# The first two up-projection units of an FFN, block by block in two PSUM banks, where a residual sum becomes the FFN's input

## The reference

```python
def rmsnorm(x, g):
    xf = x.astype(jnp.float32)
    y = xf * lax.rsqrt(jnp.mean(xf * xf, axis=-1, keepdims=True) + RMS_EPS)
    return (y * g.astype(jnp.float32)).astype(x.dtype)

def swiglu(h, w_gate, w_up, w_down):
    return (jax.nn.silu(h @ w_gate) * (h @ w_up)) @ w_down

def second_block(x, norm_g, ...):
    h = x
    for layer in range(DEPTH_2):
        g = norm_g[layer]
        u = rmsnorm(h, g[0])
        m = mixer_fox_nsa(u, ...) if layer % 2 == 0 else mixer_pool(u, ...)
        h = h + rmsnorm(m, g[1])
        u = rmsnorm(h, g[2])
        h = h + rmsnorm(swiglu(u, ffn_w_gate[layer], ffn_w_up[layer], ffn_w_down[layer]), g[3])
    return h
```

## Time and profile before

| | us |
|---|---|
| median of 3 runs | 1926.87 |
| the three runs | 1917.62, 1926.87, 1940.65 |
| span of the profiled execution, first to last instruction | 1930.8 |
| TensorE busy in it | 1849.1 (96%) |
| VectorE busy | 832.7 (43%) |
| ScalarE busy | 687.0 (36%) |
| mean granted TensorE clock | 0.949 |

### The profile page before, as it was taken

The page is one execution under the profiler, slowest core; times in us unless marked ns, Lnnn a source line. Parts: engine busy times, 40 slices in busy tenths (PEclk is TensorE's granted clock), DMA queues, the critical chain, the costliest instruction groups (busy, mean ns, idle before and its releaser), DMA issues.

```text
span 1930.8 us, 22596 instructions
## 1 busy us (share of the span) xinstructions
PE 1849.1 (96%) x8378; PEld 1431.2 (74%) x8378; DVE 832.7 (43%) x1244; ACT 687.0 (36%) x1124; POOL 30.4 (2%) x86
## 2 busy tenths in 40 slices
PE   8899889999999999999998899999998899999996
PEld 6576677888878887666666778888886678888885
DVE  3444256777743342321223354444323654444323
ACT  4533335444422223443334343332222633333221
POOL 1000000000000200000000000000002000000000
PEclk9999699999999998896897999999999899999998
DMA  4111022223332431000000212223321022223221
GB/s 156 55 44 44 22 79 83 100 87 107 104 105 86 109 111 34 12 23 11 23 23 11 88 56 97 98 98 110 105 90 66 22 73 93 96 98 114 102 78 43
DMA packets 37761, 142.72 MB, mean 74 GB/s; under 512 B 4496, under 2 KB 4656, under 8 KB 37440
## 3 DMA queue, kind: packets, MB, share of 16 engines
q1 hardware_dynamic: 36288, 138.43, 21.1%
q0 software_dynamic: 688, 2.31, 0.6%
q10 hardware_dynamic: 720, 1.10, 0.2%
HBM read 139.72 MB, written 2.10 MB: 73 GB/s over the span
## 4 chain that ended last, share of the span: by engine, by line
PE 90%; DVE 5%; ACT 3%; issue 2%; DMA 0%; DVEq 0%; ACTq 0%
PE ps L1301 25%; PE ps L1302 24%; PE ps L1303 24%; PE ps L1590 4%; PE ps L1626 3%; PE ps L1602 2%; DVE x L962 1%; DVE hlo L945 1%; PE ps L1426 1%; ACT hhi L549 1%; PE ps L1533 1%; DVE mt L956 1%; PE ps L1675 1%; PE ps L1706 1%; PE ps L1391 1%
## 5 line engine op out<-in xcount | busy, mean ns | idle before, releaser
L1301 PE MATMUL ps<-hhi,whi 128*128 128x512 f32 x1520 | 623.2, 410 | 40.7 <-DVE hlo L945 24.0
L1302 PE MATMUL ps<-hlo,whi 128*128 128x512 f32 x1520 | 600.5, 395 | 0.0
L1303 PE MATMUL ps<-hhi,wlo 128*128 128x512 f32 x1520 | 600.2, 395 | 0.0
L821 DVE TENSOR_TENSOR wlo<-raw,whi 128x1024 fp32r<-128x1024 f32 (+1 forms) x240 | 313.4, 1306 | 585.4 <-ACT whi L446 582.9
L446 ACT ACTIVATE whi<-raw 128x1024 fp32r<-128x1024 f32 (+1 forms) x240 | 269.4, 1122 | 621.9 <-PE ps L1303 621.6
L1301 PEld LDWEIGHTS ps<-hhi,whi 128*128 128x128 f32 x1520 | 290.7, 191 | 127.0 <-issue 42.5
L1303 PEld LDWEIGHTS ps<-hhi,wlo 128*128 128x128 f32 x1520 | 290.4, 191 | 62.7
L1302 PEld LDWEIGHTS ps<-hlo,whi 128*128 128x128 f32 x1520 | 290.9, 191 | 61.0 <-issue 6.4
L1301 PE MATMUL ps<-ahi,whi 128*128 128x512 f32 x528 | 209.5, 397 | 0.2 <-DVE wlo L821 0.2
L1303 PE MATMUL ps<-ahi,wlo 128*128 128x512 f32 x528 | 209.3, 396 | 0.0
L1302 PE MATMUL ps<-alo,whi 128*128 128x512 f32 x528 | 209.3, 396 | 0.0
(11 more groups left out here) (244 smaller groups left out, 1343.2 us busy)
## 6 DMA issues: line engine op xcount, KB each, us to landing
raw<-w_up_b SPq DMA_DIRECT2D x88, 512.0 KB, 3.5
raw<-w_up_a SPq DMA_DIRECT2D x44, 512.0 KB, 3.5
raw<-w_down_b SPq DMA_DIRECT2D x32, 704.0 KB, 4.0
raw<-w_in_b SPq DMA_DIRECT2D x23, 512.0 KB, 3.5
raw<-w_down_a SPq DMA_DIRECT2D x16, 704.0 KB, 3.9
raw<-w_in_a SPq DMA_DIRECT2D x19, 512.0 KB, 3.4
raw<-w_out_a SPq DMA_DIRECT2D x8, 512.0 KB, 3.5
raw<-w_out_b SPq DMA_DIRECT2D x8, 512.0 KB, 3.4
```

The lines of the kernel that those rows point to most:

```text
L821: dve.tensor_tensor(wlo[n % SPL][:, 0:cols], raw[n % RAW][:, 0:cols], whi[n % SPL][:, 0:cols].bitcast(f32), ALU.subtract).then_inc(lo_done, 1)
L1301: pe_.matmul(out, wh, hi, start=start, stop=False)
L1302: pe_.matmul(out, wh, lo, start=False, stop=False)
L1303: return pe_.matmul(out, wl, hi, start=False, stop=stop)
```

## The change

At `up_b0` and `up_b1` TensorE takes units 0 and 1 together: for each block k it waits for the operand, does the three products of unit 0 into bank 0, the three of unit 1 into bank 1, and then the square sum of the block. Both units signal `unit_done` behind their last block, unit 0 three products ahead of unit 1, and the last square sum follows. Ahead of the first block it now waits for the split weights of both units. The other phases, the other engines and the number of instructions of each kind are as before.

```diff
+            def two_units(p, e):
+
+                for k in range(KD):
+                    operand_ready(p, k)
+                    for u in range(2):
+                        last = block_mm(p, u, k, u, k == 0, k == KD - 1)
+                        if k == KD - 1:
+                            last.then_inc(unit_done, 1)
+                    squares(e, k)
+
             def gemm(p):
@@
                     e = RSTD_OF.get(p)
+                    if p in ("up_b0", "up_b1") and u < 2:
+
+                        if u == 0:
+                            pe_.wait_ge(lo_done, n + 2)
+                            two_units(p, e)
+                        return
```

## The result

| | before | after |
|---|---|---|
| median of 22 runs | 1925.18 us | 1937.88 us |
| lowest and highest | 1903.34, 1943.79 | 1918.53, 1954.39 |
| ratio | | 1.0078, 95% interval 1.0047 to 1.011 |
| profiled execution: span (own time) | 1930.8 | 1952.3 (1954.01) |

The ratio compares only the fast runs (those within 1.5% of the fastest run of the same kernel), so it isn't the ratio of the two medians (1.0066). The change makes the kernel slower by 0.8%, some 15 us, with an interval of 9 to 21 us; the medians lie 12.7 us apart. The two profiled spans are 21.5 us apart, and half of that is not the change's: 11.1 us lie ahead of the first boundary, where both programs are the same. What the change does is read from the boundaries alone.

The account below looks back on a forecast made before the run. TensorE, with 90% of the chain, was taken as the bound. Boundaries +6.3 us (a 4.4 us gain already in it) and clock +3.9 make +10.2 on 1926.87, stated as 1937.0 us; range 1925 to 1950, 8 times in 10.

Parts of the forecast that it names:

- Which chain is uncovered: Both boundaries, behind the last square sum: Ln, Exp, table load and two splits lose their cover; TensorE pauses 5.07 us.
- The blocks: TensorE at both boundaries: six products and a square sum take 2.23 us per block, with no wait between blocks.
- The second boundary's first part: First product to last square sum, 1538.78 to 1558.5: 17.8 us of blocks, 0.13 weight load, 1.75 for the low clock.
- The price of the clock: Behind the new pause at each boundary: the clock falls, costing 1.95 us each, +3.9 us for two.
- the clock is left alone: Rival, behind the new pauses: the clock does not fall, so only +6.3 us, 1933.2; chance 0.1.
- It stays low long after both pauses: Rival, behind both new pauses: the low clock costs 6.8 us in all, so +13.1 us, 1940.0; chance 0.15.
- The sum: Whole kernel: +6.3 us from both boundaries and +3.9 us from the clock, +10.2 us or 0.5%.
- The absolute time: Whole kernel: three-run median of 1926.87 us plus 10.2 us, stated as 1937.0 us.
- One reading: First FFN, kernel before: with two more table loads, unit 2's first product starts 6.3 us after the square sum ends.
- ScalarE held back by the square sums: Rival, operand ring at the boundaries: six squares held 0.6 us each and TensorE too, +3.6 us a boundary; chance 0.03.
- The Trainium skill's drain: Table-set switch in the uncovered chain: a rule adding about 1380 ns, making the sum about 2.8 us more.

Follow-up runs that it names:

- e1: The changed kernel with ScalarE's split of unit 2's weights put ahead of Ln, Exp and the table load: 1934.47 us against 1917.45, ratio 1.0073; boundaries 27.56 and 27.32 us.
- e2: The changed kernel with each block's square sum ahead of its six products: boundaries 31.89 and 30.92 us, pause 3.77 us.
- e3: The changed kernel with five unread products of ones with x put behind the last square sum to fill the pause: boundaries 31.21 and 30.46 us.
- e4: The kernel before, with only the split of unit 2's weights put ahead of Ln, Exp and the table load: boundaries 27.48 and 27.51 us.
- e7: The kernel before with the change made at the second boundary alone: boundaries 27.50 and 33.34 us.
- e8: The kernel before under another name, same instructions: ratio 1.0035 (0.9985 to 1.0085); boundaries 27.49 and 27.47 us.
- e6: Against the kernel before, three blocks of unit 1 put between unit 0's blocks, ScalarE's order unchanged: boundaries 28.29 and 27.75 us.

## Why the prediction was right

- **Which chain is uncovered** was right. Pause 5.16 us at both boundaries, forecast 5.07; e1 and e2 shortened it by the order alone, e3 left it and filled it.
- **The blocks** were right: 2.25 us apart, forecast 2.23, and no wait between them. From the first product to the end of the last sum the first boundary took 20.5 us (1121.93 to 1142.46), forecast 20.35.
- **The second boundary's first part** was too short in the sum: 21.1 us (1554.14 to 1575.27) against 19.7. The low clock lasted until about 1560.3, 6.2 us behind the first product, not 3.5. It is no cost of the change, for it lasts differently long in each execution. But the changed order pays for it, and the old order doesn't. In the old order a boundary has a length of 27.47 to 27.51 us in all seven cases of four profiles (before, e4, e7, e8), with slow stretches (the time at the low clock behind the first product) from 3.5 to 5.8 us, since its waits for `hlo` absorb the difference. In the changed order half of the slow stretch goes into the time. The windows over the first 8 us of a boundary, both of the changed kernel and the second of e3, give the slow stretch as (1 - clock) x 16 us:
```profile
1121.93:1129.93 8.00, 8.00 (x21) 0.69 0.00 0
1554.14:1562.14 8.00, 8.00 (x19) 0.61 0.01 2
1553.71:1561.71 8.00, 8.00 (x25) 0.79 0.01 2
```
(these rows have TensorE alone: length, busy time, clock, DMA share, GB/s), and from the start of unit 2 (us behind the first product) less half of it the same is left each time, to 0.1 us:

| changed order | slow stretch | start of unit 2 | less half the slow stretch |
|---|---|---|---|
| changed, first | 5.0 | 25.67 | 23.2 |
| changed, second | 6.2 | 26.28 | 23.2 |
| e3, first | 5.0 | 25.68 | 23.2 |
| e3, second | 3.4 | 24.94 | 23.3 |
| e7, second | 3.5 | 25.04 | 23.3 |

The prediction knew that half of the slow stretch is lost, and took the stretches of one profile, 4.8 and 3.5 us, as fixed.
- **The price of the clock** behind the new pause was 1.5 and 1.8 us, 3.3 in all, for 3.9 forecast. Over all pauses of this study in which the clock fell it was 1.5, 1.8, 1.7, 1.7 (e2) and 2.8 us (e7), with a mean of 1.9, so the forecast of 1.95 us each was right in its size; how much a single pause costs it could not tell. The rival "the clock is left alone" is out. "It stays low long after both pauses", at 3.4 us each, didn't happen in the profile after, but at the one pause of e7 2.8 us of the 3.4 did.
- **The sum**: +6.3 + 3.9 = +10.2 forecast, +11.3 at the boundaries, +15 (9 to 21) in whole times. Of the 11.3, 3.3 are the clock behind the pause (e3), and some 8 the pause less the gain ahead of it, 1.4 of them the slow start of the second boundary. The whole times alone would not have told the forecast from its rival of +13.1; the boundaries do.
- **The absolute time** was luck in part: 1937.0 forecast and 1937.88 measured. The forecast stood on a median of three runs of the kernel before; its median was 1925.18 in the 22 runs here, and 1917.45, 1928.25 and 1922.18 in the later comparisons, so a hit within 1 us means nothing.
- **One reading** was wrong and cost nothing: at the first FFN not two more table loads lie behind the square sum, but one. ScalarE loads at 297.63 and at 299.57; the third load of that stage, at 291.56, is over before the square sum ends. The 6.35 us there are the 5.07 of this chain and one more load of 1.28, so the row bears the forecast of the pause out better than the prediction said.
- **ScalarE held back by the square sums**: it was, by 1.0 to 1.3 us at each of six squares of the first boundary and up to 1.8 at the second, and TensorE never waited for it. That rival is out.
- **The Trainium skill's drain** behind a table load ("ScalarE: Activation LUTs", "What ACT_TABLE_LOAD costs") isn't in the trace after either: the load starts at 1143.85 and the split at 1145.14. With the page's 1380 ns of drain the pause would have been about 6.5 us, an estimate from the page's figure; it was 5.16.

## What to carry to other kernels

Work that looks like a late remainder (here unit 1 behind unit 0) may be the only cover of a serial chain on another engine; before it is moved forward, measure that chain, and move no more than what leaves it covered, or shorten the chain first by putting what TensorE waits for ahead of what it doesn't (the split ahead of `Ln`, `Exp` and the table load). An edit of less than 1% is judged by the length of its own stage, read between two instructions that both kernels have, and not by the median of whole runs.

## What was not expected of the hardware

The same instructions ahead of the first boundary took from 1091.1 to 1122.1 us over the profiles of this study, 2.8%, with the granted clock as the visible difference (0.79 to 0.86 in the second attention stage). And the low clock followed a pause of 3.77 us (e2) as it did those of 4.5 to 5.2, while behind pauses of 1.75 us (e6), 1.01 us (e1) and 0.87 us (e3) the products ran at the full clock. Two pauses of the same length need not cost the same: 5.16 us each, and 1.5 us lost behind one, 2.8 behind another (e7). In e2 the clock fell only 1.4 us after TensorE had started again.
